# One matmul of 512 columns over both parts of the input for the rounded weights of heads 1 to 7, and VectorE adding the halves of the bank

## The reference, cut to what matters

```python
q, k, v, ... = split(xn @ w_in)          # per head 128 columns of each
merged = (sigmoid(g_a) * (out_a @ w_branch_a) + sigmoid(g_b) * (out_b @ w_branch_b)
          + sigmoid(g_c) * (out_c @ w_branch_c))
x = x + merged @ w_out
x = x + hierarchical_moe(rms_norm(x, ffn_norm), ...)     # top-2 experts in the top group of 32
x = x + sigmoid(rms_norm(x, ple_norm) @ w_ple_gate) * (p @ w_ple_proj)
```

## Time and profile before

| | |
|---|---|
| median of three runs | 2166.15 us (2165.89 to 2166.63) |
| profiled execution | 2163.43 us |
| its span, first to last instruction | 2161.7 us |
| PE, PEld, DVE, ACT, POOL busy | 1806.0, 1358.3, 854.9, 690.7, 196.5 us |
| mean granted TensorE clock | 0.939 of full speed |
| DMA | 593.01 MB, mean 274 GB/s |
| chain that ended last | PE 56%, DMA 34%, ACT 4% |

### The profile page before, as it was taken

One profiled execution on the slowest core, in us unless ns is written; L12 is line 12 of the kernel. 1 busy time (PEld: TensorE's weight loads), 2 busy tenths in 40 slices (PEclk: granted clock), 3 DMA queues, 4 the chain that ended last, 5 costly groups with the idle time before them and its releaser, 6 DMA issues.

```text
span 2161.7 us, 42213 instructions
## 1 busy us (share of the span) xinstructions
PE 1806.0 (84%) x17850; PEld 1358.3 (63%) x17851; DVE 854.9 (40%) x1387; ACT 690.7 (32%) x952; POOL 196.5 (9%) x172
## 2 busy tenths in 40 slices
PE   5999999999889999998978776667666667666699
PEld 5899999999768888887854433333333333333367
DVE  2364445554444554444433332222222222222274
ACT  3356555666553333343331100101000101000173
POOL 4332333233200000000000000000000000000000
PEclk9999999999989999999989989898889998888899
DMA  8455444455325555555867999999999999999972
GB/s 165 128 146 135 130 132 127 118 135 136 117 83 193 193 193 195 194 184 211 330 234 310 426 424 426 425 426 427 427 425 426 426 427 428 426 426 426 425 276 92
DMA packets 258898, 593.01 MB, mean 274 GB/s; under 512 B 31514, under 2 KB 171034, under 8 KB 225306
## 3 DMA queue, kind: packets, MB, share of 16 engines
q1 hardware_dynamic: 258842, 592.19, 73.5%
HBM read 590.07 MB, written 2.10 MB: 274 GB/s over the span
## 4 chain that ended last, share of the span: by engine, by line
PE 56%; DMA 34%; ACT 4%; SPq 2%; DVE 1%; DVEq 1%; issue 1%; ACTq 1%
DMA ring<-in_w_e_down 33%; PE bank L711 21%; PE bank L506 15%; PE bank L892 4%; PE bank L950 4%; PE bank L865 2%; ACT ring L1004 1%; SPq L296 1%; ACT L1004 1%; PE bank L618 1%; PE bank L851 1%; DMA ring<-in_w_in 1%; PE bank L911 1%; PE bank L842 1%; DVEq L1325 1%
## 5 line engine op out<-in xcount | busy, mean ns | idle before, releaser
L1004 ACT ACTIVATE wh<-ring 128x2048 fp32r<-128x2048 f32 x156 | 298.4, 1913 | 252.6 <-DMA ring<-in_w_in 127.2
L865 PE MATMUL bank<-ring,mo 128*32 128x128 f32 x6144 | 214.2, 299 | 136.7 <-DMA ring<-in_w_e_up 116.2
L865 PEld LDWEIGHTS bank<-ring,mo 128*32 128x32 f32 x6144 | 185.7, 120 | 180.0 <-DMA ring<-in_w_e_up 145.8
L1543 DVE TENSOR_TENSOR wl<-ring,wh 128x2048 fp32r<-128x2048 f32 x86 | 197.1, 2292 | 232.6 <-ACT wh L1004 232.5
L1004 ACT ACTIVATE mo<-bank 128x128 f32<-128x128 f32 (+2 forms) x145 | 47.7, 334 | 622.6 <-PE bank L879 309.3
L892 PE MATMUL bank<-ring,mo 128*32 128x512 f32 x1024 | 166.7, 785 | 89.1 <-DMA ring<-in_w_e_down 84.3
L461 POOL TENSOR_TENSOR wl<-ring,wh 128x512 fp32r<-128x512 f32 x132 | 170.2, 1320 | 365.2 <-ACT wh L1004 365.2
L506 PE MATMUL bank<-xh,wh 128*128 128x256 f32 x1088 | 160.4, 295 | 3.1 <-ACT xh L1004 3.1
L506 PE MATMUL bank<-xl,wh 128*128 128x256 f32 x1088 | 156.9, 291 | 4.5 <-POOL xl L448 4.5
L1712 DVE TENSOR_TENSOR x_tok<-x_tok,bank 128x512 f32<-128x512 f32 x256 | 158.1, 679 | 0.0
L892 PEld LDWEIGHTS bank<-ring,mo 128*32 128x32 f32 x1024 | 34.5, 127 | 187.3 <-DMA ring<-in_w_e_down 93.4
(11 more groups left out here) (353 smaller groups left out, 2377.0 us busy)
## 6 DMA issues: line engine op xcount, KB each, us to landing
ring<-in_w_e_down SPq DMA_DIRECT2D x64, 2048.0 KB, 26.1
ring<-in_w_e_up SPq DMA_DIRECT2D x64, 2048.0 KB, 26.4
ring<-in_w_in SPq DMA_DIRECT2D x116, 1024.0 KB, 5.5
ring<-in_w_e_gate SPq DMA_DIRECT2D x32, 2048.0 KB, 30.6
xnT<-in_w_e_gate SPq DMA_DIRECT2D x16, 2048.0 KB, 29.5
mo<-in_w_e_gate SPq DMA_DIRECT2D x16, 2048.0 KB, 33.9
ring<-in_w_out SPq DMA_DIRECT2D x16, 1024.0 KB, 5.1
ring<-in_w_ple_gate SPq DMA_DIRECT2D x8, 2048.0 KB, 14.7
```

The costliest lines, as they stand in the source:

```text
L865: m = mm(bank[b][32 * j:32 * j + 32, 0:P], xw[:, 8 * (i % 2) + k, :], m_gu[piece][:, k, j * P:j * P + P], start=(i % 2 == 0 and k == 0), s ...
L1004: return act.activation(out, in_, func, **kw)
L1543: tt(ul[u % PAIRS], unit_slot[u % PAIRS], uh[u % PAIRS], ALU.subtract).then_inc(sem("u_lo"), 1)
```

## The change

- `xh` and `xl` become the two halves of one tensor `xhl` at the same addresses.
- For heads 1 to 7 `wide` takes the place of `dense`. The product `wh xh` and the product `wh xl` are one: 16 matmuls of 512 columns, whose moving operand is block i of `xh` and of `xl`; the first sum goes to the left half of the bank, the second to the right. `wl xh` follows as 16 matmuls of 256 columns into the left half. The four quarters have 6, 6, 8 and 12 matmuls, of which 6, 6, 4 and 0 are wide.
- The bank's halves still have to be added. VectorE does it while it copies the tile out: `add_halves` is a sum over a pair of elements 256 apart, 512 elements in, 256 out. ScalarE no longer evacuates in the loop, and waits for `raw` where it reads `raw_sb` and `raw_sw`.
- The eight `evac` calls stand at new places, in VectorE's `mix`.

```diff
+        xhl = nc.alloc_sbuf_tensor_at("xhl", [P, 2, KT, S], F32R, offset=x_tok_at)
+        xh, xl = xhl[:, 0], xhl[:, 1]
...
+            PIECES = ((0, 6), (6, 12), (12, 20), (20, 32))
+
+            def wide(h, q, hold):
...
+                s = q // 4
+                p, to = s % PAIRS, bank[s % 2]
+                if q % 4 == 0:
+                    pe.wait_ge(*event("raw", 8 * h + s - 1))
+                    pe.wait_ge(*event("w_hi", 8 * h + s + PRO + 1))
+                for i in range(*PIECES[q % 4]):
+                    if i == KT:
+                        pe.wait_ge(*(event("v_lo", 4 * h + s // 2 + 3) if s % 2 == 0 else event("w_lo", 4 * h + s // 2 + 3)))
+                    if hold and i == PIECES[q % 4][1] - 1:
+                        hold()
+                    if i < KT:
+                        m = mm(to[:].rearrange("p (a n) -> p a n", a=2), wh[p][:, i, :], xhl[:, :, i, :], start=(i == 0), stop=False,
+                               skip_group_check=True)
+                    else:
+                        m = mm(to[:, 0:S], wl[p][:, i - KT, :], xh[:, i - KT, :], start=False, stop=(i == 2 * KT - 1),
+                               skip_group_check=True)
+                if q % 4 == 3:
+                    m.then_inc(sem("tile_mm"), 1)
...
-                mix(h - 1, h, lambda q, hold=None: dense(h, q, hold))
+                mix(h - 1, h, lambda q, hold=None: wide(h, q, hold))
...
             def mix(n, evac, hi, sigmoid_conv):
                 act.drain()
+                act.wait_ge(*event("raw", 8 * n - 2))
                 f(sq_sb, raw_sb[:, :, :].rearrange("p a s -> p (a s)"), ACT.Square).then_inc(sem("sb_sq"), 1)
                 act.wait_ge(*event("dn_silu", n))
                 f(sq_dn, cv[:, 0:2 * S], ACT.Square).then_inc(sem("dn_sq"), 1)
+                act.wait_ge(*event("raw", 8 * n))
                 f(sq_sw, raw_sw, ACT.Square).then_inc(sem("sw_sq"), 1)
...
-                mix(h, lambda s: evacuate(s, h), lambda s: hi(h, s), lambda: conv_sig(h + 1))
+                mix(h, lambda s: None, lambda s: hi(h, s), lambda: conv_sig(h + 1))
...
+            def add_halves(s, h):
...
+                dve.wait_ge(*event("tile_mm", 8 * h + s + PRO + 1))
+                dve.tensor_reduce(to, bank[s % 2][:].rearrange("p (a n) -> p n a", a=2), AX.X, ALU.add).then_inc(sem("raw"), 1)
...
+                evac(0)
                 lo(2)
...
                 lo(3)
+                evac(1)
...
                 ts(smx[:, P:3 * P], smx[:, P:3 * P], sm[:, 11:12], None, ALU.mult).then_inc(sem("sw_pr"), 1)
+                evac(2)
                 lo(4)
...
+                    if r == 3:
+                        evac(3)
...
                 dve.tensor_copy(inv[BLOCKS[0], :, CH:P], x_psum).then_inc(sem("dn_inv"), 1)
+                evac(4)
                 lo(6)
...
+                evac(5)
                 lo(7)
                 dve.wait_ge(*event("dn_v", 2 * n))
                 dve.tensor_copy(vn[:, P:S], bank[6][:, P:S]).then_inc(sem("dn_vn"), 1)
+                evac(6)
                 lo(8)
+                evac(7)
                 dve.wait_ge(*event("dn_ort", n))
```

More of the change, by code:

```diff
@@ L212, in hybrid_trunk @@
         unit_slot = [ring[:, 2048 * i:2048 * i + 2048].rearrange("p (t n) -> p t n", t=4) for i in range(PAIRS)]
-        xh = nc.alloc_sbuf_tensor_at("xh", [P, KT, S], F32R, offset=x_tok_at)
-        xl = nc.alloc_sbuf_tensor_at("xl", [P, KT, S], F32R, offset=xnT_at)
+        assert xnT_at == x_tok_at + 4 * KT * S
+        xhl = nc.alloc_sbuf_tensor_at("xhl", [P, 2, KT, S], F32R, offset=x_tok_at)
+        xh, xl = xhl[:, 0], xhl[:, 1]
         wh = [nc.alloc_sbuf_tensor_at(f"wh{p}", [P, KT, P], F32R, offset=ring_at + 8192 * (PAIRS + p)) for p in range(PAIRS)]
@@ L1074, in decay_rows, with evacuate @@
                 act.drain().then_inc(sem("Gb"), 1)
-            def evacuate(s, h):
+            def evacuate(s):
                 to = (raw_dn[:, 0, 3:], raw_dn[:, 1, 3:], raw_dn[:, 2, 3:], raw_v, raw_sb[:, 0, :], raw_sb[:, 1, :],
                       raw_z, raw_sw)[s]
-                act.wait_ge(*event("tile_mm", 8 * h + s + PRO + 1))
+                act.wait_ge(*event("tile_mm", s + PRO + 1))
                 f(to, bank[s % 2][:, 0:S], ACT.Copy).then_inc(sem("raw"), 1)
@@ L1177, in _ @@
                 hi(0, s + 2)
-                evacuate(s, 0)
+                evacuate(s)
                 if 1 <= s < 5:
@@ L1432, in silu, with mix @@
                 tt(cv, cv, ex, ALU.mult).then_inc(sem("dn_silu"), 1)
-            def mix(n, next_tap, next_silu, lo):
+            def add_halves(s, h):
+                to = (raw_dn[:, 0, 3:], raw_dn[:, 1, 3:], raw_dn[:, 2, 3:], raw_v, raw_sb[:, 0, :], raw_sb[:, 1, :],
+                      raw_z, raw_sw)[s]
+                dve.wait_ge(*event("tile_mm", 8 * h + s + PRO + 1))
+                dve.tensor_reduce(to, bank[s % 2][:].rearrange("p (a n) -> p n a", a=2), AX.X, ALU.add).then_inc(sem("raw"), 1)
+            def mix(n, next_tap, next_silu, lo, evac):
                 one = ds(n - 1, 1)
@@ L1538, in _ @@
             with dve.Fori(1, NH) as h:
-                mix(h, lambda j: tap(j, h + 1), lambda: silu(h + 1), lambda s: lo(s % PAIRS, 8 * h + s + PRO) if s % 2 == 0 else None)
+                mix(h, lambda j: tap(j, h + 1), lambda: silu(h + 1), lambda s: lo(s % PAIRS, 8 * h + s + PRO) if s % 2 == 0 else None,
+                    lambda s: add_halves(s, h))
             def unit_lo(u):
@@ L1547, in first_units @@
                     unit_lo(u)
-            mix(NH, lambda j: None, lambda: None, first_units)
+            mix(NH, lambda j: None, lambda: None, first_units, lambda s: None)
             def prod(i):
```

## The result

The changed kernel takes 2152.59 us, the median of 6 runs (2149.63 to 2155.7), beside 2165.53 us (2162.55 to 2166.63) for the kernel before in as many runs: a ratio of 0.9943, with a 95% interval of 0.993 to 0.996. That is 12.9 us less, where 17.0 were forecast. The profiled run took 2150.88 us with a span of 2149.1.

What follows compares the result with a forecast made beforehand. The prediction took TensorE's own instruction stream to bound heads 1 to 7. It summed 11.96 - 2.05 + 5.8 + 1.27 = 17.0 us, taken off 2166.15 us to give 2149.2 us, range 2146 to 2157.

Steps and rivals of the forecast that it cites:

- its own case: Whole kernel: both parts gain as costed, 2149.2 us, own range 2146 to 2152, chance 0.64.
- rivals near 2156: VectorE paces the rounds (2156.2 us, chance 0.12), or ScalarE's gain is missing (2156.3 us, chance 0.06).
- 5.8 us: Boundaries of heads 2 to 7: without ScalarE's evacuation, L549 to L556 shrinks to 2.65 us, 0.96 us each.
- 1.27 us: Last head: L549 itself waits for ScalarE, so the whole 1.27 us of its earlier chain comes forward.
- 896 x 13.35 ns = 11.96 us: Heads 1 to 7: merging 896 matmul pairs saves each pair one fixed cost of 13.35 ns.
- sixteen wide ones at 226.7 ns: Sign that the forecast is right: a tile's sixteen wide matmuls run at a pitch of 226.7 ns.
- Slower: Rival: the operand's second run, 16 KB behind the first, stalls TensorE; 2350 us at twice the pitch; chance 0.06.
- each run of 256 pays the whole cost (240 ns): Rival: wide matmuls take 240 ns and save nothing or little; only ScalarE's 7.1 us remain, 2159.1 us; chance 0.10.
- What does not land.: Three places per head paced by other engines: 0.29 us of the matmul saving is lost there, 2.05 us in seven.
- I cost these at nothing.: VectorE's eight reduces a head, about 0.65 us each, fit its idle time and cost TensorE nothing.
- 1.13 us of room: VectorE ahead of the first tap, held by POOL's first operation: room for evac(2)'s reduce of 0.65 us.
- the second rival: VectorE paces the rounds: reduce over 1.13 us or held by GpSimd, taps slip, 7 us back, 2156.2; chance 0.12.

Runs made afterwards that it cites:

- e1: Changed kernel with the 256-column matmuls kept narrow and VectorE copying the tiles out instead of summing halves; ratio 0.9955 to the kernel before.
- e3: Kernel before with only tile 7's evacuation in heads 1 to 7 moved from ScalarE to VectorE, as a copy; ratio 0.9964 to the kernel before.
- e4: Changed kernel with the wide matmul's moving operand as one contiguous run of 512, for time alone (other sums); ratio 0.9942 to the kernel before.
- e7: Changed kernel with a second, unused sum over the whole bank ahead of each of VectorE's reduces; 2162.25 us, ratio 0.9979 to the kernel before.
- e10: Changed kernel with each reduce's sum doubled and the next head's first tap moved directly behind tile 2's evacuation; 2156.84 us, ratio 0.996.

## Why the prediction came out as it did

The direction was right, and both parts of the change do what they were said to do; the gain was forecast 4 us too large, all of it in one term. 2152.59 us lies in the stated range of 2146 to 2157, but 0.6 us outside the 2146 to 2152 that the forecast gave its own case: the range had been widened for rivals near 2156 that didn't come true, so that it holds is in part luck. By the steps:

- **ScalarE, "5.8 us" and "1.27 us".** Right. L574 to L581 is 2.60 us (2.65 forecast), 1.01 us in each of six heads; e1 measures the whole part at 7.34 us against 7.07. That the load waits for no semaphore shows in the row at 183.64, and that the copy ahead of it was the whole cause in e3.
- **Wide matmuls, "896 x 13.35 ns = 11.96 us".** This term was mis-sized. From e1 to the changed kernel it is 440.45 - 434.45 = 6.00 us up to the last L574, and 444.06 - 437.85 = 6.21 up to the last L581, where 11.96 - 2.05 = 9.9 were forecast. The price came from 63 groups that follow each other without a break, but the heads cut the stream into pieces of 6 to 16. The prediction's own sign, sixteen wide ones at 226.7 ns, didn't come: they take 3.86 us behind L700, 241 ns each, with single pitches that settle at 227. Behind a break wide ones run over their steady pitch and narrow ones under it: the piece above saves 0.03 instead of 0.08, the 16 behind L700 0.15 instead of 0.214. Summed over all pieces of a head, e1's less the changed kernel's, that gives 0.90 us of the 0.91 by which the period fell, where 1.71 - 0.29 = 1.42 was forecast. e4 rules out the second run of the operand, the rival called "Slower"; that each run of 256 pays the whole cost (240 ns) is ruled out by the 227 too. What in the chip makes the pitches behind a break isn't settled.
- **"What does not land."** Right. L581 to L585 kept 2.64 us and L615 to L631 its 5.87.
- **"I cost these at nothing."** Right for seven of the eight reduces (0.68 us, forecast 0.65). At the last boundary TensorE does wait for the eighth: tile 7's reduce ends at 561.21 + 0.69 = 561.90, and TensorE stands 0.35 us for it until 561.96. There no quarter of another tile follows to cover it. From L700 to L574 it is 3.85 us against 3.64 in e1, 0.21 us more. But L581 waits for ScalarE there, and from L700 to L581 it is 7.25 us in both kernels, so even this wait costs nothing in the end. VectorE in the changed kernel, then TensorE in e1:

```profile
561.21 0.69 DVE L1466 TENSOR_REDUCE mo<-bank 128x256 f32<-128x512 f32 x1 [2.91 <-PE bank L554]
```

```profile
569.61 0.59 PE L700 MATMUL bank<-ring,ones 128*128 128x256 f32 x2
...
573.25 1.12 PE L574 MATMUL bank<-ring,ones 128*128 128x512 f32 x2
...
576.86 1.10 PE L581 MATMUL bank<-ring,ones 128*128 128x512 f32 x2 [1.57 <-ACT ring L1029]
```

- **"1.13 us of room".** Wrong as a reading, without effect on the time. It looked only at the first tap, which is held to GpSimd's end anyway. The copy `hc` ahead of it isn't held as long as it starts before GpSimd, which in the changed kernel it does by 0.10 us. e7 moved it to 0.50 us behind GpSimd's start and lost 1.38 us a head: the second rival's mechanism is real, and it costs more than the 1 us a head that was put on it. The rival's condition, an evacuation of over 1.13 us, was met in e7 too (0.60 + 0.68 = 1.28 us), and no run has a value between 0.68 and that. That the loss would already begin some 0.10 us above 0.68 is an estimate from the row at 215.09, and isn't shown.

The rule of the Trainium skill, "SBUF — State Buffer", section "SBUF: two separate sides", was weighed for the reduce alone. The trace agrees on that: 21 of the 56 reduces in the heads run beside a GpSimd operation and take 0.68 us, as the other 35 do. The copy of 12 elements, 1.06 us beside GpSimd and 0.16 without it, would fit the rule as an operation in a two-port mode; no row shows in which mode it ran. In the Trainium skill, the section "Back-to-back issue gap" of "TensorE: Matmul & The Clock Gate" has the formula by which merging a pair is worth 2.5 ns (2.2 us in all); the section calls it the gap of an isolated matmul and not that of a stream. As a price for this stream it is contradicted by e1 against the changed kernel: 6.00 us over the 896, 6.7 ns a pair.

## What to carry to other kernels

Take the price of an instruction from rows where it stands as it will stand: merging two matmuls saved 13.35 ns by the unbroken streams, 6.7 ns over the heads, their waits included, and 4 in the piece of six shown. When you measure the room of an engine, follow the first instruction behind the new work, not the one that is slow already; here it was a copy of 12 elements. And look at what stands ahead of a table load: moving one 0.39 us copy off ScalarE gave over half of this change's gain.

## What was not expected of the hardware

- Matmuls behind a break, first pitch left out: with 512 columns 224 to 236 ns for the next six to nine and then 227; with 384 columns 171 to 177 in most pieces, up to 185 in two; with 256 columns (e1) 113 to 125, under 120 in the mean, and then 120. Contiguous or strided makes no difference with 512 columns.
- A reduce over two halves of a bank, read with a step of 256 elements, takes 0.68 us; the sum over 512 adjacent elements takes 0.68 too (row at 212.30 of e10, 128x1 from 128x512). No cost of the step shows.
- Beside GpSimd's operations, each tap on VectorE lasts as long as one of them (1.29 us); without, three take 0.88 us.
